# Splitting the weight stream of a two-layer fp32 decoder trunk by pieces of 2048 columns instead of units of 1024

## The reference

```
h = x
h = h + retention_branch(rms_norm(h, ret_norm), ret_w_in, ret_w_out)      # layer 0
h = h + sigmoid(rms_norm(h, ple_norm[0]) @ ple_w_gate[0]) * (p[0] @ ple_w_proj[0])
h = h + pool_branch(rms_norm(h, pool_norm), pool_w_in, pool_w_group, scale, pool_w_out)   # layer 1
h = h + sigmoid(rms_norm(h, ple_norm[1]) @ ple_w_gate[1]) * (p[1] @ ple_w_proj[1])
return rms_norm(h, final_norm)

# retention: q, k, v, g = split(xn @ w_in); rotate q, k; per head (q k^T * decay) v, normalise;
#            (silu(g) * y) @ w_out
# pooling:   u, g = split(xn @ w_in); d = window means of u, less u; mixed = (d @ w_group) * scale;
#            (mixed * silu(g)) @ w_out
```

## Time and profile before

| | us |
|---|---|
| median of 3 runs | 1606.74 (1606.66 to 1607.39) |
| the profiled execution | 1606.02 |
| its span, first to last instruction | 1604.2 |
| TensorE busy | 1583.2 (99%) |
| VectorE busy | 989.0 (62%) |
| ScalarE busy | 727.1 (45%) |
| DMA | 188 GB/s mean over the span |

### The profile page before, as it was taken

One profiled execution on the slowest core, in us unless ns is written; L12 is line 12 of the kernel. 1 busy time (PEld: TensorE's weight loads), 2 busy tenths in 40 slices (PEclk: granted clock), 3 DMA queues, 4 the chain that ended last, 5 costly groups with the idle time before them and its releaser, 6 DMA issues.

```text
span 1604.2 us, 19551 instructions
## 1 busy us (share of the span) xinstructions
PE 1583.2 (99%) x7218; PEld 1315.9 (82%) x7218; DVE 989.0 (62%) x1220; ACT 727.1 (45%) x889; POOL 5.1 (0%) x13
## 2 busy tenths in 40 slices
PE   8999999999999999999999999999999999999997
PEld 6788888888888888888888888888888888888885
DVE  6675666657566666757756555645565555556565
ACT  6444434344443444445655444334434443445553
POOL 0000000000000000000000000000000000000000
PEclk9999999999999999999999999999999999999999
DMA  9544554545445554545455555555544555454551
GB/s 387 206 168 179 185 196 168 193 168 187 183 180 183 183 183 162 204 183 203 165 190 206 186 184 174 194 184 185 183 184 181 204 187 185 179 213 184 184 186 77
DMA packets 43670, 301.34 MB, mean 188 GB/s; under 512 B 4944, under 2 KB 4960, under 8 KB 8176
## 3 DMA queue, kind: packets, MB, share of 16 engines
q1 hardware_dynamic: 41840, 294.14, 50.4%
q0 software_dynamic: 1072, 5.06, 0.8%
q10 hardware_dynamic: 720, 1.61, 0.3%
HBM read 298.70 MB, written 2.10 MB: 188 GB/s over the span
## 4 chain that ended last, share of the span: by engine, by line
PE 97%; DMA 2%; DVE 1%; SPq 1%; issue 0%; ACT 0%; POOL 0%; DVEq 0%
PE accB L314 11%; PE accB L315 11%; PE accB L316 11%; PE accC L314 10%; PE accC L315 10%; PE accC L316 10%; PE accA L314 10%; PE accA L315 10%; PE accA L316 10%; PE side L337 2%; DMA h<-in_x_dram 1%; DMA ropes<-in_rope_dram 1%; PE side L375 0%; PE side L374 0%; PE side L376 0%; PE side L443 0%
## 5 line engine op out<-in xcount | busy, mean ns | idle before, releaser
L843 DVE TENSOR_TENSOR w_lo<-w_raw,w_hi 128x1024 fp32r<-128x1024 f32 x551 | 668.6, 1223 | 420.4 <-ACT w_hi L592 416.2
L592 ACT CAST w_hi<-w_raw 128x1024 fp32r<-128x1024 f32 x551 | 578.5, 1054 | 619.9 <-PE accB L316 263.8
L314 PE MATMUL accA<-w_hi,xa_hi 128*128 128x512 f32 x508 | 198.8, 391 | 0.0
L315 PE MATMUL accA<-w_lo,xa_hi 128*128 128x512 f32 x508 | 197.7, 389 | 0.0
L316 PE MATMUL accA<-w_hi,xa_lo 128*128 128x512 f32 x508 | 197.7, 389 | 0.0
L314 PE MATMUL accC<-w_hi,xa_hi 128*128 128x512 f32 x384 | 150.9, 393 | 0.0
L315 PE MATMUL accC<-w_lo,xa_hi 128*128 128x512 f32 x384 | 149.7, 390 | 0.0
L316 PE MATMUL accC<-w_hi,xa_lo 128*128 128x512 f32 x384 | 149.5, 389 | 0.0
L314 PE MATMUL accB<-w_hi,xa_hi 128*128 128x512 f32 x384 | 149.4, 389 | 0.0
L315 PE MATMUL accB<-w_lo,xa_hi 128*128 128x512 f32 x384 | 149.4, 389 | 0.0
L316 PE MATMUL accB<-w_hi,xa_lo 128*128 128x512 f32 x384 | 149.4, 389 | 0.0
(11 more groups left out here) (196 smaller groups left out, 2124.0 us busy)
## 6 DMA issues: line engine op xcount, KB each, us to landing
w_raw<-in_stream_dram SPq DMA_DIRECT2D x275, 1024.0 KB, 4.8
h<-in_x_dram SPq DMA_DIRECT2D x4, 512.0 KB, 15.8
xT_raw<-in_xT_dram SPq DMA_DIRECT2D x3, 512.0 KB, 10.2
dec<-in_decay_dram POOLq DMA_DIRECT2D x1, 1024.0 KB, 16.4
fgain<-in_final_gain_dram POOLq DMA_DIRECT2D x1, 1024.0 KB, 5.2
out_dram<-emb ACTq DMA_DIRECT2D x2, 512.0 KB, 3.1
out_dram<-emb SPq DMA_DIRECT2D x2, 512.0 KB, 2.7
bnd_raw<-in_band_dram POOLq DMA_DIRECT2D x1, 768.0 KB, 6.3
```

The source lines that it names most:

```text
L314: pe.matmul(acc[pair][t][:], xh, wh, start=first and b == 0, stop=False)
L315: pe.matmul(acc[pair][t][:], xh, wl, start=False, stop=False)
L592: act.copy(w_hi[:, r % RING, :], w_raw[:, r // 2, (r % 2) * 1024:(r % 2 + 1) * 1024]).then_inc(hi_ready, 1)
L843: dve.tensor_tensor(w_lo[:, r % RING, :], w_raw[:, r // 2, (r % 2) * 1024:(r % 2 + 1) * 1024], w_hi[:, r % RING, :].bitcast(F32), ALU.subt ...
```

## The change

`split_hi` and `split_lo` work on a whole piece at even units, with one instruction of 128 x 2048 each, and count two on their semaphore; at odd units they issue nothing. The pair's cast waits until both places are free: `unit_used` >= u + 2 - 4. Unit 1 keeps an instruction of its own, as unit 0 does. TensorE's program is the same, and so are SyncE's waits and the places in the code at which side work stands.

```
 def split_hi(u, base, seg, landings):
     r = (seg + u) % (2 * RAW)
-    if u % 2 == 0 or (isinstance(base, int) and base + u == 1):
+    if isinstance(base, int) and base + u == 1:
+        act.wait_ge(w_landed[0], landings(u))
+        act.copy(w_hi[:, 1, :], w_raw[:, 0, UNIT * COL:]).then_inc(hi_ready, 1)
+    elif r % 2 == 0:
         act.wait_ge(w_landed[r // 2], landings(u))
-    if not (isinstance(base, int) and base + u < RING):
-        act.wait_ge(unit_used, base + (u + 1 - RING))
-    act.copy(w_hi[:, r % RING, :], w_raw[:, r // 2, (r % 2) * 1024:(r % 2 + 1) * 1024]).then_inc(hi_ready, 1)
+        if not (isinstance(base, int) and base + u < RING):
+            act.wait_ge(unit_used, base + (u + 2 - RING))
+        act.copy(w_hi[:, r % RING:r % RING + 2, :], w_raw[:, r // 2, :].rearrange("p (u n) -> p u n", u=2)
+                 ).then_inc(hi_ready, 2)

 def split_lo(u, base, seg):
     r = (seg + u) % (2 * RAW)
-    dve.wait_ge(hi_ready, base + (u + 1))
-    dve.tensor_tensor(w_lo[:, r % RING, :], w_raw[:, r // 2, (r % 2) * 1024:(r % 2 + 1) * 1024],
-                      w_hi[:, r % RING, :].bitcast(F32), ALU.subtract).then_inc(lo_ready, 1)
+    if isinstance(base, int) and base + u == 1:
+        dve.wait_ge(hi_ready, 2)
+        dve.tensor_tensor(w_lo[:, 1, :], w_raw[:, 0, UNIT * COL:], w_hi[:, 1, :].bitcast(F32), ALU.subtract
+                          ).then_inc(lo_ready, 1)
+    elif r % 2 == 0:
+        dve.wait_ge(hi_ready, base + (u + 2))
+        dve.tensor_tensor(w_lo[:, r % RING:r % RING + 2, :],
+                          w_raw[:, r // 2, :].rearrange("p (u n) -> p u n", u=2),
+                          w_hi[:, r % RING:r % RING + 2, :].bitcast(F32), ALU.subtract).then_inc(lo_ready, 2)
```

## The result

| | before | after |
|---|---|---|
| median of the runs compared | 1606.7 (1605.94 to 1607.39, 4 runs) | 1658.04 (1654.75 to 1663.3, 4 runs) |
| the profiled execution | 1606.02 | 1660.65 |
| its span | 1604.2 | 1658.8 |
| mean granted clock | 0.996 | 0.988 |

After to before is 1.0326 [1.0313, 1.0338]: slower by 51 us. The forecast was 1651, with a range of 1640 to 1664; its narrow case ended at 1656. The four runs of after lie 8.5 us apart, those of before 1.5.

A forecast was written before the change was run, and what follows sets the result against it. TensorE, busy 99% of the span, was taken to bound the kernel. 1606.02 + 39.1 of waits + 5.6 for clock falls = 1650.7, put at 1651 for the runs' median; own range 1648 to 1656, 8 in 10 1640 to 1664.

The forecast's parts named there:

- The late release, and what stands behind a split: A pair's cast waits one unit longer; plain stretches keep 0.86 us spare, but instructions queued behind a split come later.
- the second rival: Clock falls at all eight closing waits, or some shorter ones too: 8 to 15 falls, 1657 to 1667; chance 0.15.
- Closings, 8 x 3.07: Both layers' closings: TensorE's transposes wait 3.07 us for VectorE's addition into h, eight times, 24.6 us.
- Gating 4 x 1.55, layer 1 3 x 1.64, groups 4 x 0.35: Waits for gated h, 6.2 us; layer 1's next pair after ScalarE's squares, 4.9; the gate's product at groups, 1.4.
- Start 1.6: First units: unit 2's pair is ready 1.5 us late, and the rotation's transposes come at 43.9 instead of 42.24.
- Waits, sum 39.1: All added TensorE waits: 24.6 + 6.2 + 4.9 + 1.4 + 1.6 + 0.4 us.
- Heads hidden: Seven retention heads cost nothing: behind the rotation the next split ends 0.2 us early, normalising has some 0.1 spare.
- the third rival: Long split instructions exceed their slopes by more than the 0.86 us spare, so every pair pays: 1680 and up; chance 0.07.
- The clock, 4 falls x 1.4 = 5.6: Half of the eight closing waits make TensorE's clock fall, 1.4 us each; the shorter waits bring none.
- The first rival: The clock holds through all the waits: 1646; chance 0.25.
- Not slower, by a closer spacing: Halving the splits gives back up to 7 ns per matmul, 46 us, paying for the waits: about 1600; chance 0.06.
- Half of the waits absorbed: Something wrongly placed in the order absorbs half of the waits, above all at the eight closings: 1634; chance 0.07.

The follow-up runs named there:

- e3: Kernel before with its short splits; only the cast of an even unit waits until both places of its pair are free: 1619.6, ratio 1.0085.
- e1: Changed kernel with the additions into h in both closings put ahead of the pair's split (8 places): 1625.24, ratio 1.0121.
- e4: Changed kernel with side work TensorE waited for put ahead of the wide splits, layer 1's squares later, units 2 and 3 split singly: 1609.33, ratio 1.0022.
- e5: Changed kernel with VectorE's subtraction back at 1024 columns per instruction, ScalarE's cast still at 2048: 1631.37, ratio 1.0158.
- e2: Changed kernel with 12 matmuls whose result is overwritten in each of TensorE's eight waits for the addition into h: 1651.36, ratio 1.0283.
- e9: e8 with the rotation's tables loaded when the first chunk of x has landed instead of the last: 1606.96, ratio 1.0008.
- e6: Changed kernel with units of 1024 in the two closings alone, wide splits kept in heads and groups: 1613.05, ratio 1.0042.
- e8: Kernel before with dec and p loaded only after the rotation's tables have landed, and the row scale one unit earlier: 1606.22, ratio 0.9999.

## Why the prediction was right, and where it was off

**The late release, and what stands behind a split.** Right, and the cause: e3 shows the release alone making waits at the same eight places, e1 takes them away by order alone, e4 nearly everything.

The measured 1658 lies in the range of 8 in 10, but 2 us above the forecast's own range (1648 to 1656), in the band that the second rival had. No two errors cancelled: waits and clock were both put too low.

**Closings, 8 x 3.07.** 8 x 2.96 by the trace. An idle time in the trace is counted from the modelled end of the last matmul, 0.39 us behind its start, where the next would have started 0.227 behind it; so a wait takes 0.16 us more than it shows, 3.12. The links were each right: 1.91 and 2.29 for the splits, 1.28 for the additions.

**Gating 4 x 1.55, layer 1 3 x 1.64, groups 4 x 0.35.** By the trace 1.43 to 1.46; 1.56, 1.59 and 1.85; and 0.21 to 0.24. With 0.16 added to each, the three sums are within 0.6 us of the forecast. One place in layer 1 reads:

```profile
1581.56 0.63 ACT L608 ACTIVATE junk<-h 128x512 bf16<-128x512 f32 x1 [3.69 <-DVE h L992]
1582.81 1.89 ACT L595 CAST w_hi<-w_raw 128x2048 fp32r<-128x2048 f32 x1
1584.80 2.29 DVE L852 TENSOR_TENSOR w_lo<-w_raw,w_hi 128x2048 fp32r<-128x2048 f32 x1 [1.94 <-ACT w_hi L595]
1587.15 0.50 PE L314 MATMUL accC<-w_hi,xb_hi 128*128 128x512 f32 x1 [1.59 <-DVE w_lo L852]
```

ScalarE's two squares wait for h, the cast waits behind them, and a wait of the side work turns into one of the stream.

**Start 1.6.** The transposes came at 44.15; forecast 43.9, before 42.24. The wait showed as 1.47 us at 16.52 and the rest by the rotation, as put. Not foreseen was a half clock of 6.8 instead of 3.4 us.

**Waits, sum 39.1.** 46.9 - 9.7 = 37.2 us in the trace, and 22 or so waits more or longer at 0.16: 40.8. Behind each, work is slower than before by 0.06 us (16 sets of transposes, 1.09 instead of 1.03) or 0.1 (five first products on w_lo, 0.33 to the next start instead of 0.227): 1.5 us that the sum did not have.

**Heads hidden.** 92.3 us each instead of 92.26 (one 92.5), 0.6 us over all. The thin margins held. In e5, where the split of unit 11 stands behind the rotation, they didn't.

**Lengths of the splits.** 1.92 and 2.30 forecast, 1.909 and 2.292 found; the third rival is out.

**The clock, 4 falls x 1.4 = 5.6.** This is the term that was mis-sized. Seven falls cost 11.3, 1.6 each, and the longer half clock at the start 0.8: 12.1. Another way: (1 - clock) x span is 0.012 x 1658.8 = 19.9 after and 0.004 x 1604.2 = 6.4 before, 13.5 apart, of which 1.5 lie in idle time (0.6 in the two falls, 0.9 at the start). The idle part that the forecast took off each fall was there in two of the seven only; the others began when TensorE was at work again (the window 758 to 759 above). So 40.8 + 1.5 + 12.1 = 54.4, where 54.6 were found. The forecast read two half clocks in the trace of before; there is a third, from 1598.1 on, 5.2 us behind TensorE's last product, which costs nothing and in which the clock held for longer than 3 us too.

The number of falls isn't a constant of the kernel. The four runs have granted clocks of 0.991, 0.991, 0.988 and 0.987, in the order of their times, 1654.75 to 1663.3. The trace, with seven falls, is the run of 0.988. Worked out from it, the others had about four, four and eight (an estimate: 1.7 us of (1 - clock) x span for each fall, 8.0 us of it elsewhere). The forecast's own case, "some falls", thus holds in two of four runs, and these are 4 us above the 1651 for the waits and costs named here; the median lies above them because of the other two, which fit the second rival, "nearly everywhere". The first rival, no falls, would be e2's clock without its filling, and didn't come. Which waits bring a fall stays open.

By the Trainium skill ("TensorE: Matmul & The Clock Gate", section "Why this matters for your kernels") it is gaps over about 3 us that send the clock down. The order of size agrees: behind eight waits of 1.8 us (e5) and eight of 0.9 to 1.2 (e3) it held. As an edge it doesn't: of eight waits shown as 2.96 us six had a fall and two hadn't, two of the six falls came 2.3 and 2.4 us into the wait, and one wait of 1.85 was followed by one.

**Not slower, by a closer spacing.** The matmuls are 0.227 us apart after as before, with half the splits. So the 14 ns don't come from the number of split instructions or their semaphores, here; where they come from no run shows. That rival is out.

**Half of the waits absorbed.** None was.

## What to carry to other kernels

Longer instructions on an engine off the critical path saved nothing here, and they moved the time at which a buffer is asked for and the time at which everything queued behind them is done. Before merging two instructions, list whom the bounding engine waits for and put those ahead of the merged one in the order: e1 and e4 took back 33 and 48 of 51 us in that way. A row of short waits on TensorE can cost far more than it shows: 37 us of waits came to 54 here, 12 of the difference by the clock. A wait that can't be removed can be filled with matmuls, which held the clock in e2.

## What the runs showed of the hardware that was not expected

- The fall of the clock at nearly equal idle times isn't the same each time: at six of eight waits of 2.96 us in one execution, two of these falls while TensorE was still idle; at none of eight of 1.8 (e5); at one of seven of 1.4 to 1.9 in the changed kernel, and at none of the same seven in e1 and e2. At the start a wait that ends at 7.9 to 8.0 is followed by a fall in e9 (2.23 us) and by none in e3 and e4 (2.33 us). A kernel with such waits has a spread of its own: 8.5 us here over four runs, against 1.5 over four runs of the kernel before and 2.9 over 27.
- Half the clock lasted 3.4 us in each of the seven falls. Behind the rotation of the first head it lasted 3.4 in the kernel before, e5 and e9, and 6.8 in the changed kernel, e1 to e4 and e6 to e8. Eight transposes of fp32 lead in there as they do at the closings; why it is 3.4 in one and twice that in another was not found.
- An idle time that the trace shows for TensorE is 0.16 us short of what the wait costs, since the modelled ends of matmuls reach over the next one's start. Over 22 waits that is 3.6 us. The work right behind a wait took 0.06 to 0.1 us more, another 1.5 us.
- From the cast's end to the subtraction's start were 0.10 us (752.59 + 1.91 to 754.60), where before there were 0.03.
